# Residual operand splits one position later, and one load ahead of two stores, in the feed-forward stage of a hybrid attention trunk

## The reference

```python
mix = jnp.concatenate([od, orr], axis=-1)
x = x + jnp.einsum('bse,ed->bsd', mix, w_out[l])           # (2048, 1024) by (1024, 1024)
h = rms_norm(x, ffn_norm_g[l])
ff = jax.nn.silu(jnp.einsum('bsd,df->bsf', h, w_gate[l])) * jnp.einsum('bsd,df->bsf', h, w_up[l])
x = x + jnp.einsum('bsf,fd->bsd', ff, w_down[l])            # d_ff is 2816
```

## Time and profile before

| | |
|---|---|
| median of 3 runs | 2736.29 us (2734.64 to 2737.57) |
| the profiled execution, device time | 2737.57 us |
| its span, first to last instruction | 2735.9 us |
| mean granted TensorE clock | 0.986 |
| PE busy | 2613.9 us, 96% |
| weight loads (PEld) busy | 2211.9 us, 81% |
| DVE busy | 1553.7 us, 57% |
| ACT busy | 1142.9 us, 42% |
| POOL busy | 905.1 us, 33% |
| HBM traffic | 158 GB/s over the span |

### The profile page before, as it was taken

How to read it: one execution, slowest core, us unless ns; L and a number is a source line. 1 busy time by engine, 2 the same in 40 slices (tenths; PEclk the granted TensorE clock), 3 DMA queues, 4 the chain that set the end, 5 groups by cost and what they waited for, 6 DMA issues and landing times. The chain is left out here.

```text
span 2735.9 us, 34330 instructions
## 1 busy us (share of the span) xinstructions
PE 2613.9 (96%) x13288; PEld 2211.9 (81%) x13288; DVE 1553.7 (57%) x1915; ACT 1142.9 (42%) x1917; POOL 905.1 (33%) x607
## 2 busy tenths in 40 slices
PE   7999999999999999987999999999999996999999
PEld 6888888887888889885877888887888885888887
DVE  5434344333676767676567666667656664356653
ACT  4434344332576766775554222324222222322231
POOL 5001100002424141403546554554545551236300
PEclk9999999999999999998999999999999998999999
DMA  4755555384343433306784433335333334777763
GB/s 158 261 188 198 169 196 203 121 283 130 104 108 109 108 100 94 109 29 214 234 282 145 115 96 104 105 102 193 104 113 101 115 86 145 252 267 275 244 204 129
DMA packets 343874, 430.48 MB, mean 157 GB/s; under 512 B 19232, under 2 KB 212768, under 8 KB 341024
## 3 DMA queue, kind: packets, MB, share of 16 engines
q1 hardware_dynamic: 343712, 428.29, 49.6%
HBM read 301.87 MB, written 129.50 MB: 158 GB/s over the span
## 5 line engine op out<-in xcount | busy, mean ns | idle before, releaser
L2297 PE MATMUL down_prod<-down_w_hi,down_f_hi 128*128 128x512 f32 x616 | 241.0, 391 | 21.0 <-DVE down_f_lo L2233 20.2
L549 DVE TENSOR_TENSOR proj_w_lo<-proj_w_raw,proj_w_hi 128x2048 fp32r<-128x2048 f32 x56 | 129.7, 2316 | 230.4 <-ACT proj_w_hi L449 230.4
L696 PE MATMUL proj_prod<-proj_w_hi,proj_h_lo 128*128 128x512 f32 x640 | 250.3, 391 | 0.0
L2298 PE MATMUL down_prod<-down_w_lo,down_f_hi 128*128 128x512 f32 x616 | 240.4, 390 | 0.0
L2299 PE MATMUL down_prod<-down_w_hi,down_f_lo 128*128 128x512 f32 x616 | 240.3, 390 | 0.0
L1742 ACT ACTIVATE feed_a_hi<-lend_shared 128x1024 fp32r<-128x1024 f32 (+1 forms) x78 | 93.8, 1202 | 290.3 <-PE feed_v_bank L2023 142.0
L1087 ACT ACTIVATE att_expo<-att_ring,att_neg_max 128x1024 f32<-128x1024 f32 (+4 forms) x192 | 164.7, 862 | 92.7 <-DVE att_neg_max L1203 74.7
L2203 ACT ACTIVATE down_f_hi<-down_f_raw 128x768 fp32r<-128x768 f32 x112 | 82.8, 785 | 282.8 <-PE down_prod L2299 279.6
L2021 PE MATMUL feed_y_bank<-feed_b_hi,feed_a_hi 128*128 128x512 f32 x416 | 165.5, 398 | 15.9 <-DVE feed_results L1889 15.9
L2021 PE MATMUL feed_x_bank<-feed_b_hi,feed_a_hi 128*128 128x512 f32 x416 | 163.3, 392 | 13.0 <-DVE lend_lent L1858 11.0
L1742 ACT ACTIVATE feed_a_hi<-feed_full 128x1024 fp32r<-128x1024 f32 (+1 forms) x78 | 93.5, 1202 | 185.8 <-PE feed_y_bank L2023 136.9
(11 more groups left out here) (266 smaller groups left out, 6855.2 us busy)
## 6 DMA issues: line engine op xcount, KB each, us to landing
proj_w_raw<-in_w_in_dram SPq DMA_DIRECT2D x56, 1024.0 KB, 6.5
lend_shared<-in_w_gate_dram SPq DMA_DIRECT2D x88, 256.0 KB, 4.0
feed_full<-in_w_up_dram SPq DMA_DIRECT2D x88, 256.0 KB, 4.0
ff<-feed_results SPq DMA_DIRECT2D x88, 256.0 KB, 2.5
down_w_raw<-in_w_down_dram SPq DMA_DIRECT2D x22, 1024.0 KB, 7.5
down_f_raw<-ff SPq DMA_DIRECT2D x56, 384.0 KB, 3.3
down_f_raw<-ff SPq DMA_DIRECT2D x56, 320.0 KB, 3.4
ff<-feed_ff_sum SPq DMA_DIRECT2D x66, 256.0 KB, 3.2
```

Source lines behind the costliest of these rows:

```text
L549: nc.vector.tensor_tensor(w_lo[n % 2][:], w_raw[n % 2][:], w_hi[n % 2][:].bitcast(F32), ALU.subtract).then_inc(w_lo_made, 1)
L696: last = pe.matmul(prod[t][:], lo[:, s, tile], wh[:, k, :], start=False, stop=stop)
L2297: pe.matmul(dst, hi[:, s, :], wh[:, s, :], start=opens and s == 0, stop=False, skip_group_check=True)
L2298: pe.matmul(dst, hi[:, s, :], wl[:, s, :], start=False, stop=False, skip_group_check=True)
```

## The change

Three things are moved; nothing is added to or taken from the work.

1. In the closing groups 7 and 29 the splits of the next set's B operands 0, 1, 2 (`high_b` on ACT, `low_b` on DVE) stand at pos 4, 5, 6 instead of pos 3, 4, 5. At pos 6 of group 7 `high_b` of operand 2 stands behind `root(7, 1)`.
2. In the opening groups 0, 8 and 30 `high(g+1, 0)` and `low(g+1, 0)` stand behind pos 6 instead of at pos 5. In group 0 nothing else stands between the two places; in 8 and 30 the sigmoids and `use` of pos 5 and 6 do.
3. On SP, `load_a(g+2)` at pos 0 stands ahead of `store_t(turns(g-1), 2, 4)`. Both exist in one group only: 9.

```diff
-        EARLY = {3: 0, 4: 1, 5: 2}
+        EARLY = 3
         LATE = {0: (3,), 2: (4,), 3: (5,), 4: (6,)}
@@ sync
                         if p is not None:
                             store_x(p)
+                        elif g + 2 < GROUPS and not closes_set(g):
+                            load_a(g + 2)
                         if turns(g - 1) is not None:
                             store_t(turns(g - 1), 2, 4)
-                        if p is None and g + 2 < GROUPS and not closes_set(g):
-                            load_a(g + 2)
@@ scalar
-                    if opens_set(g) and pos == 5:
-                        high(g + 1, 0)
                     if g >= OUT_GROUPS and not is_up(g):
...
                     if pos == 6 and 0 < g < OUT_GROUPS:
                         root(g, 1, TILE22)
-                    if closes_set(g) and pos in EARLY:
-                        high_b(set_of(g) + 1, EARLY[pos])
+                    if closes_set(g) and pos >= OPERANDS - EARLY:
+                        high_b(set_of(g) + 1, pos - (OPERANDS - EARLY))
                 if opens_set(g):
+                    high(g + 1, 0)
                     high(g + 1, 1)
@@ vector
-                    if opens_set(g) and pos == 5:
-                        low(g + 1, 0)
...
-                    if closes_set(g) and pos in EARLY:
-                        low_b(set_of(g) + 1, EARLY[pos])
+                    if closes_set(g) and pos >= OPERANDS - EARLY:
+                        low_b(set_of(g) + 1, pos - (OPERANDS - EARLY))
                 if opens_set(g):
+                    low(g + 1, 0)
                     low(g + 1, 1)
```

## The result

The changed kernel takes 2753.98 us (median of 4 runs, 2752.69 to 2754.47) against 2735.47 us for the kernel before beside it: ratio 1.0066, 95% interval [1.0055, 1.0079], 18.1 us slower by the ratio. Timed once more on another occasion it was 2754.51 against 2739.77 us, ratio 1.0055 [1.0043, 1.0067], 15.1 us. So 15 us is probably the better figure. One execution of the kernel before, at 6779.09 us, is slow for a reason that the record doesn't give, and is left out of the ratios. The forecast was 2748.5 us, 2742 to 2754.

The account below looks back on a forecast made before the run. PE, busy nearly all the time, was taken as the bound, its waits deciding. Terms 9.1 (group 9, including 2.4 from group 8) + 1.5 (clock) + 0.9 (group 31) = 11.5 us slower; forecast 2748.5 us, range 2742 to 2754.

Parts of the forecast that it names:

- Rival 2: Two slow positions follow both long waits, in groups 8 and 9, and landings are at their latest: 2751 to 2752 us; 15%.
- the upper bound of the landing: Group 9: the two stores land by 1478.3, after the loads at 1477.1 with the same latency once more; 1477.3 was taken.
- Group 7: make_c22 starts at 1425.4 and PE starts position 6 at 1426.1 in place of 1427.94: 1.8 us won.
- Group 8: high_b 2 and low_b 2 add 4.1 us between root and scale; PE's position 3 comes 2.4 us late.
- Group 9, the splits: A operand splits on DVE: low(9, 2) ends 2.4 us later, at 1471.2 instead of 1468.8.
- Group 9, the store behind the loads: Stores of T2 and T4 land at 1477.3 behind load_a(11); PE 9.1 us late, 6.7 of it from the queue.
- The clock: After group 9's wait of some 7 us, position 3 costs 4.4 us in place of 2.9: 1.5 us more.
- position 0 of group 9 is swallowed by position 3: PE's first position of group 9 waits about 1.2 us for low(9, 0), which position 3 would have waited anyway.
- Group 31: POOL's chain from sums(31) to make_u2(31) moves by 0 to 1.9 us; 0.9 us taken.
- The rival that only the queue counts: Group 7's gain lives, group 8 gives -1.8 instead of +2.4, landing at its lower bound: 2741.6 to 2742.5 us; 12%.
- The rival that the clock takes more: Rival 2: two slow positions after both long waits, about 1 us more each in groups 9 and 8; 2751 to 2752; 15%.
- The rival that `copy_first` isn't held by T2 and T4: Group 9: the swap costs nothing, group 7 gives 1.8 us and full clock 1.7 us: 2733 to 2736 us; 3%.

Follow-up runs that it names:

- e6: Kernel before with the B splits of operands 0 and 1 one position later in groups 7 and 29, operand 2 staying at position 5: ratio 1.0004.
- e1: Kernel before with only the SP queue order changed, load_a(11) ahead of the stores of T2 and T4 in group 9: ratio 1.0032.
- e5: Kernel before with SP waiting for low(9,2) ahead of the stores of T2 and T4, loads still behind the stores: ratio 1.0031.
- e7: Kernel before with the B splits of operands 0, 1, 2 one position later in group 29 alone: ratio 1.0000.
- e11: Kernel before with the later B splits and the swapped SP queue, but high and low of batch 0 left at position 5: ratio 1.0051.
- e2: Kernel before with only the B splits of operands 0, 1, 2 one position later in groups 7 and 29: ratio 1.0018.
- e4: Kernel before with the later B splits and batch 0 behind position 6, SP queue as before: ratio 1.0022.
- e8: Kernel before with high_b and low_b rearranged at the border of groups 7 and 8, no split between root and scale on ACT: ratio 0.9987.
- e10: Kernel before with only POOL's gate in group 8 opened earlier, sums(9) waiting for low_b 3 instead of low_b 5: ratio 1.0003.

## Why the prediction was right, and what it mis-sized

The direction and the mechanism hold: the kernel is slower through the chain from `root` to `scale` in group 8 and through the stores behind the loads in group 9. The sum was too small, 11.5 us where 15.1 and 18.1 were measured. That the first median, 2753.98, lies inside the range is luck: it is 0.02 us from the end, and the end of 2754 doesn't follow from the prediction's terms. Rival 2, from which it is said to come, has the upper bound of the landing in it already and reaches 2751 to 2752.

Up to position 4 of group 9 the prediction had 9.1 + 1.5 = 10.6 us, and said that all later starts would be shifted by 10 to 11. They are shifted by one constant, as said, but by 18.1 and 13.9 us in the two traces of the changed kernel. Point by point:

- **Group 7**: counted from the mark `make_c22` comes 1.6 us earlier, PE's wait is 1.8 us instead of 3.4; forecast 1.8 and 1.6 less. Right.
- **Group 8**: position 3 was to be 2.4 us late through the chain from `root` to `scale`; 2.2 to 3.0 in the traces with all of part 1 in group 7, and e6 shows that it is that chain. Right. In the changed kernel's trace `root` comes 1.6 us earlier (forecast 1.7) and the chain is 4.8 us longer (forecast 4.1; `low_b` 2 took 3.12 us and not 2.2).
- **Group 9, the splits**: `low(9, 2)` was to end 2.4 us late. From the mark it ended at 50.0 before, 55.9 and 53.5 in the two traces of the changed kernel: 5.9 and 3.4. Much of that is scatter: it is 49.8 to 51.2 in the four kernels that are as before up to there (before, e1, e5, e7), 52.2 and 54.1 with part 1 (e11, e2), and 53.5 to 55.9 with parts 1 and 2. The means of these say 2.7 us for part 1, near the forecast, and about 1.4 more for part 2, which the prediction put at nothing. The slow clock behind the 8 us wait in group 8 (5.19 us for position 3 at 0.51, 4.42 before) and `low(9, 0)` behind three `use` point the same way; how much each does is not shown.
- **Group 9, the store behind the loads**: from the end of `low(9, 2)` to `copy_first` the sum had 6.1 us; it was 8.2 in e1, 8.3 in the repetition and 9.2 in the first trace, 2.1 to 3.1 more. This is the mis-sized term that stands clear of the scatter. The stores were taken to land just behind the loads, 3.4 us after their issue; the one that counts took 5.3 to 6.2. The bound from above, 1478.3 in place of 1477.3, was one more us and still too low: the traces' 8.2 to 9.2 us are 1479.4 to 1480.4 on the prediction's axis. (Nor does 1478.3 follow from its words; 1473.9 and the loads' 4.1 us are 1478.0.) e5 shows both halves: from the end of `low(9, 2)` it is 4.6 us with the wait alone, and 3.6 more with the loads in front. Why the landings are slower there is not shown.
- **The clock**: 1.5 us was forecast behind the wait of group 9; 5.12, 5.03 and 4.24 us for that position (changed, e1, repetition) instead of 2.89 are 2.2, 2.1 and 1.4. And "position 0 of group 9 is swallowed by position 3" ignored that a wait of 2.6 to 3.9 us there also costs a slow position (4.21 and 4.44 us instead of 2.72).
- Together the misses in group 9 (`low(9, 2)`, the stores, the slow position 3) are 7.3 us in the first trace and 3.1 in the repetition, which makes 17.9 and 13.7 out of 10.6, within 0.2 of the two traces.
- **Group 31**: 0.9 us forecast, 0.8 in e7's trace, too little to be seen in its time. With part 2 as well it is 1.4 to 1.5 (changed, repetition, e4), and position 0 of group 31 waits 1.9 us there instead of 1.15.
- The rival that only the queue counts is out (e2 is slower by itself). The rival that the clock takes more has the nearest figure, but not the mechanism: its second slow position behind a wait doesn't come, position 4 of group 9 takes 2.72 to 2.76 us in every trace. The rival that `copy_first` isn't held by T2 and T4 is out by e1.

The Trainium skill's rule on the DMA semaphore (DMA: Bandwidth & Descriptors, "Queues, rings and completion order"), that an increment lands only after every earlier write of the same DMA engine, was applied to whole transfers, as a lower bound for the landing. For the later store, which `copy_first` waits for, the traces agree: in e1 the last load lands 5.0 us after its issue, at about 1475.6, and that store at 1476.8. For the earlier store they don't: in the changed kernel it is seen 1.2 us before the last load. The rule speaks of each DMA engine by itself, and no run here shows them one by one. The loads themselves had also become slower (6.0 us for the slowest in the changed kernel, 4.1 in the earlier trace rows).

## What to carry to other kernels

An in-order queue is only as early as its most patient entry: before a store that somebody waits for is put behind loads, look at what the loads wait for, and count the landing with the loads in the same queue. A step that alternates between two engines (`root`, `invert`, `scale`) pays twice for anything that is put in the middle (here 4.8 us for one operand), and gains when the waits in it are filled with work that both ends can spare, as e8 does. A wait that ends a little earlier is worth nothing where the next wait is fed by another chain (e6). And where two executions of one program differ by 4 us at one point of the trace, a split of the loss by single traces is good to a few us only, however exact the rows.

## What the runs showed of the hardware

- The position behind a wait runs at full clock or not, from one execution to another, for nearly the same wait: behind 2.15 and 2.19 us of idle time (e10, e7) position 3 of group 9 took 4.42 and 4.44 us, behind 1.93 and 3.03 us (before, e8) 2.89 and 2.90. Behind 1.85 us ahead of position 6 of group 7 it is 4.43 us in the repetition of the changed kernel and 2.87 in e4 and e8. Here are e7 and e8 (length, busy of PE, PEld, DVE, ACT and POOL, granted clock, DMA):

```profile
1469.01:1473.45 4.44, 4.44 (x12) 3.50 (x13) 1.56 (x1) 0.00 (x0) 0.48 (x1) 0.62 0.80 229
```
```profile
1469.10:1472.00 2.90, 2.90 (x13) 2.36 (x13) 1.30 (x1) 1.06 (x1) 1.78 (x2) 1.00 0.76 215
```

That is 1.5 us of noise for each such wait, and the kernel has several. A mean granted clock of 0.62 lies between the levels 1.2 GHz (0.50) and 2.4 GHz (1.00): most of the stretch was at the lower one.

- A store of 256 KB to memory landed 2.4 us after its issue alone, 2.4 to 4.1 in a pair (e5), and 4.4 to 6.2 directly behind four loads of the same size, where the first of two stores was seen 1.2 us before the last of the loads in front of it.
